# Per-layer embedding of the first token tile placed between the row lookups of the second tile

## What is computed

```python
def peer_ffn(h, ...):              # per token: 8 heads x 16 picked rows of u_tab and v_tab
    act = jax.nn.gelu(jnp.einsum('cd,ckd->ck', xc, uc))
    return jnp.einsum('ck,ckd->cd', gc * act, vc)

def per_layer_embed(h, p_i, g, w_gate, w_proj):
    gate = jax.nn.sigmoid(rms_norm(h, g) @ w_gate)      # w_gate 1024 x 1024
    return h + gate * (p_i @ w_proj)                    # p_i 256 tokens x 256, w_proj 256 x 1024

# layer i:
h = h + peer_ffn(rms_norm(h, norm_ffn[i]), ...)
h = per_layer_embed(h, p[i], norm_ple[i], ple_w_gate[i], ple_w_proj[i])
```

## Time and profile before

| | us |
|---|---|
| median of 3 runs | 3167.94 |
| lowest and highest run | 3167.43, 3169.96 |
| the profiled execution: its own time | 3172.68 |
| its span, first to last instruction | 3170.8 |
| first row loop, first lookup issued to last matmul | 186.0 to 863.8 |
| end of it to the first kv matmul | 863.8 to 923.3 |
| second row loop's last matmul to the first mix_in matmul | 1810.3 to 1879.3 |

### The profile page before, as it was taken

One profiled execution on the slowest core, in us unless ns is written; L12 is line 12 of the kernel. 1 busy time (PEld: TensorE's weight loads), 2 busy tenths in 40 slices (PEclk: granted clock), 3 DMA queues, 4 the chain that ended last, 5 costly groups with the idle time before them and its releaser, 6 DMA issues.

```text
span 3170.8 us, 28409 instructions
## 1 busy us (share of the span) xinstructions
PE 2703.6 (85%) x9642; PEld 1254.1 (40%) x9642; DVE 1345.4 (42%) x3325; ACT 581.9 (18%) x1216; POOL 487.8 (15%) x526
## 2 busy tenths in 40 slices
PE   8898777777788898777877789669999999999998
PEld 7373333333355473333333346534333333333233
DVE  3547777776521547777776420333111111111112
ACT  1112222222102312222222101301111111111111
POOL 0014333333200014333333100000000000000000
PEclk9799998999889999999899989578999999999999
DMA  4679999999625479999999623043999999899987
GB/s 173 241 288 410 421 421 421 422 421 421 287 93 186 173 303 420 421 421 421 421 421 421 261 93 143 17 167 160 385 422 422 422 422 422 353 422 422 422 362 302
DMA packets 145580, 1049.89 MB, mean 331 GB/s; under 512 B 16304, under 2 KB 16560, under 8 KB 18512
## 3 DMA queue, kind: packets, MB, share of 16 engines
q0 software_dynamic: 74064, 537.56, 40.8%
q1 hardware_dynamic: 70560, 508.59, 39.5%
q10 hardware_dynamic: 864, 2.65, 0.2%
HBM read 1047.69 MB, written 1.05 MB: 331 GB/s over the span
## 4 chain that ended last, share of the span: by engine, by line
PE 51%; DMA 37%; DVE 7%; ACT 2%; issue 1%; DVEq 1%; SPq 0%; POOL 0%; ACTq 0%; POOLq 0%
DMA big<-in_peer_uv,rows_of 20%; DMA big<-in_moe 12%; PE psum L526 11%; PE psum L806 10%; PE psum L426 9%; PE psum L438 7%; PE psum L832 5%; DMA uv_more<-in_peer_uv,rows_of 4%; DVE big L1305 2%; PE psum L721 1%; PE psum L787 1%; PE psum L800 1%; PE psum L473 1%; DMA ring<-in_ada 1%; ACT gdiag L914 1%
## 5 line engine op out<-in xcount | busy, mean ns | idle before, releaser
L526 PE MATMUL psum<-big,gdiag 128*128 128x512 f32 x1880 | 923.7, 648 | 275.3 <-ACT gdiag L914 275.3
L1305 DVE CUSTOM_DVE_ANT_0 big<-psum,big 128x1024 f32<-128x1024 f32 x470 | 575.0, 1224 | 312.8 <-DMA big<-in_peer_uv,rows_of 308.1
L526 PEld LDWEIGHTS psum<-big,gdiag 128*128 128x128 f32 x1880 | 377.9, 207 | 818.0 <-issue 442.3
L1669 POOL DMA_INDIRECT big<-in_peer_uv,rows_of x470 | 443.1, 943 | 1262.5 <-PE psum L526 762.2
L806 PE MATMUL psum<-big 128*64 128x512 f32 x2240 | 501.1, 597 | 25.0 <-POOLq L1691 24.5
L1635 DVE TENSOR_SCALAR big<-psum 128x512 f32<-128x512 f32 x35 | 24.2, 692 | 663.0 <-PE psum L806 663.0
L806 PEld LDWEIGHTS psum<-big 128*64 128x64 f32 x2240 | 152.6, 137 | 371.0 <-issue 276.6
L426 PE MATMUL psum<-big,ring 128*128 128x256 f32 x1280 | 288.8, 389 | 9.3 <-DVE big L1130 3.4
L426 PEld LDWEIGHTS psum<-big,ring 128*128 128x128 f32 x1280 | 250.0, 196 | 47.7 <-DVE big L1130 4.3
L832 PE MATMUL psum<-ring,big 128*64 128x512 f32 x1120 | 248.1, 595 | 3.9
L438 PE MATMUL psum<-ring,big 128*128 128x512 f32 x480 | 216.8, 614 | 3.3 <-DVE big L1130 2.3
(11 more groups left out here) (347 smaller groups left out, 1828.5 us busy)
## 6 DMA issues: line engine op xcount, KB each, us to landing
big<-in_moe SPq DMA_DIRECT2D x256, 1024.0 KB, 20.6
ring<-in_moe SPq DMA_DIRECT2D x128, 1024.0 KB, 19.6
ring<-in_ada SPq DMA_DIRECT2D x24, 1024.0 KB, 7.4
ring<-in_peer_wq SPq DMA_DIRECT2D x16, 1024.0 KB, 7.2
ring<-in_mix_in SPq DMA_DIRECT2D x14, 1024.0 KB, 6.2
ring<-in_a_in SPq DMA_DIRECT2D x8, 1024.0 KB, 7.4
ring<-in_ple_gate SPq DMA_DIRECT2D x8, 1024.0 KB, 9.0
ring<-in_kv SPq DMA_DIRECT2D x8, 1024.0 KB, 6.2
```

Of the source, the lines that this page charges most:

```text
L526: mm = pe.matmul(psum[:, OUT_BANK[t] + c, :], gdiag[:, n % DIAGS, :], uv[(PICKS * l + n) % ROWS][:, D + c * 512:D + (c + 1) * 512], start= ...
L1305: j = dve.tensor_tensor_reduce(out=u, in0=x, in1=u, scale=1.0, scalar=0.0, op0=ALU.mult, op1=ALU.add, accum_out=dots[:, n:n + 1])
L1669: pool.indirect_dma_start(uv[g % ROWS], None, table, bass.IndirectOffsetOnAxis(rows_of[:, n:n + 1], 0)).then_inc(uv_loaded[g % ROWS], 16)
```

## The change

For tile 0 the whole per-layer embedding is done while the rows of tile 1 are looked up. On VectorE it is a generator, `first_tile`, of which one step is taken after every fourth pick from n = 139 on, with pauses (a `yield 9` leaves eight groups of four picks out). On TensorE and ScalarE its pieces stand at fixed picks. Scratch for it lies in parts of `big` that hold the top-k scores and queries until then. `ple_proj` leaves the ring; its weights and `pT` are loaded by SP into SBUF as soon as the last product of the queries is done. Only tile 1 is left behind the loop. The row of the final norm moves from the diagonals' buffer to `big`, and is spread at pick 180.

```diff
-    ("ple_gate0", 2, "AA"), ("ple_proj0", 1, "DDDD"),
+    ("ple_gate0", 2, "A"),
...
@@ SyncE: peer(l)
-                load(FIRST[f"ple_proj{l}"], d["ple_proj"][l], words=2 * D)
+                sp.wait_ge(tile_done, ENDS[FIRST[f"peer_q{l}"] + 3])
+                sp.dma_start(proj_w, d["ple_proj"][l].rearrange("p (k f) -> p k f", k=2)).then_inc(p_loaded, 16)
+                sp.dma_start(pT, d["pT"][l]).then_inc(p_loaded, 16)
...
@@ TensorE: peer(l, i)
+                def gate_first(s):
+                    pe.wait_ge(xT_ready, 4 * (i + 1) + 4 * l + 2)
+                    for k in range(KC):
+                        mm = pe.matmul(psum[:, 6 + s, :], xT[:, k, 0:P], w[:, k, :], start=(k == 0), stop=(k == KC - 1))
+                    mm.then_inc(gate0_done, 1)
+                def project(t):
+                    for c in range(2):
+                        for k in range(2):
+                            mm = pe.matmul(psum[:, 4 + c, :], pT[:, k, t * P:(t + 1) * P],
+                                           proj_w[:, k, c * 512:(c + 1) * 512], start=(k == 0), stop=(k == 1))
+                    mm.then_inc(prod_done, 1)
                 for n in range(BATCH, PICKS):
+                    if n == 148:
+                        turn(i + 1, first, (0,))
+                    if n == 156:
+                        gate_first(0)
+                    if n == 164:
+                        gate_first(1)
+                    if n == 176:
+                        pe.wait_ge(p_loaded, 32 * (l + 1))
+                        project(0)
+                    if n == 180 and l:
+                        pe.wait_ge(gate0_ready, 4)
+                        for half in range(2):
+                            spread(half, V8("final_norm"), half, 6 + half)
+                    if n == 212:
+                        pe.wait_ge(prod_taken, 2 * l + 1)
+                        project(1)
                     mix_rows(n)
@@ TensorE: ple(l, i): tile 1 alone
+                turn(i, hs, (1,))
...
+                        mm = pe.matmul(psum[:, m % 3, :], xT[:, k, P:T], w[:, k, :], start=(k == 0), stop=(k == KC - 1))
...
+                pe.wait_ge(prod_taken, 2 * l + 2)
...
+            turn(3, first, (0,))
+            turn(3, hs, (1,))
@@ ScalarE: row loop, and behind it
+                        if at == 136:
+                            root(4 + 6 * l, 0)
+                        if at == 168:
+                            for s in range(2):
+                                act.wait_ge(gate0_done, 2 * l + s + 1)
+                                act.activation(gate0[:, s * 512:(s + 1) * 512], psum[:, 6 + s, :],
+                                               ACT.Sigmoid).then_inc(gate0_ready, 1)
+                        if at == 184:
+                            root(5 + 6 * l, 0)
+                            if l:
+                                for half in range(2):
+                                    take_row(half, row_f, half, 6 + half)
+                        if at == 188 and l:
+                            root(12, 0)
...
-                act.dma_start(pT, d["pT"][l]).then_inc(p_loaded, 16)
                 act.dma_start(late, d["late"]).then_inc(late_loaded, 16)
@@ VectorE: peer(l, i)
+                def first_tile():
+                    dve.wait_ge(v_done, PICKS * l + PICKS // TT)
+                    for c in range(2):
+                        o = h[:, 0, c * 512:(c + 1) * 512]
+                        dve.tensor_tensor(o, o, psum[:, OUT_BANK[0] + c, :], ALU.add)
+                    dve.drain()
+                    square(0, h[:, 0, :], first[:, 0, :])
+                    yield 1
+                    inverse(4 + 6 * l, 0)
+                    scaled(0, first)
+                    yield 2
+                    gains(i + 1, V8(f"norm_ple{l}"), tiles=(0,))
+                    yield 9
+                    dve.wait_ge(gate0_ready, 2 * l + 2)
+                    dve.wait_ge(prod_done, 2 * l + 1)
+                    o = gate0.rearrange("p (a b) -> p a b", a=2)
+                    dve.tensor_tensor(o, psum[:, 4:6, :], o, ALU.mult).then_inc(prod_taken, 1)
+                    dve.drain()
+                    dve.tensor_tensor(h[:, 0, :], h[:, 0, :], gate0, ALU.add)
+                    dve.drain()
+                    square(0, h[:, 0, :], first[:, 0, :])
+                    yield 1
+                    inverse(5 + 6 * l, 0)
+                    if l:
+                        dve.wait_ge(row_taken, 2)
+                        dve.scalar_tensor_tensor(h[:, 0, :], h[:, 0, :], rstd[:, 0:1], row_f, ALU.mult, ALU.mult)
+                        dve.drain()
+                        square(0, h[:, 0, :], first[:, 0, :])
+                        yield 1
+                        inverse(12, 0)
+                    scaled(0, first)
+                    yield 99
...
+                            if n >= 139:
+                                pause -= 1
+                                if pause <= 0:
+                                    pause = next(beside)
+                dve.wait_ge(v_done, PICKS * (l + 1))
+                for c in range(2):
+                    o = h[:, 1, c * 512:(c + 1) * 512]
+                    dve.tensor_tensor(o, o, psum[:, OUT_BANK[1] + c, :], ALU.add)
+                dve.drain()
+                square(1, h[:, 1, :])
+                inverse(6 + 7 * l, 1)
+                scaled(1)
```

More of the change, by code:

```diff
@@ L190, in build @@
         ple_t = region(4096, TT, D)
-        pT = region(6144, 2, T)
+        proj_w = region(24576, 2, D)
+        pT = region(26624, 2, T)
+        gate0 = region(27136, D)
+        first = region(28672, 1, D)
         xT2 = region(2048, KC, T)
@@ L440, in tokens, with turn @@
                     mm.then_inc(tile_done, 1)
-            def turn(i, src=hs):
-                for t in range(TT):
-                    pe.wait_ge(hs_ready, 2 * i + t + 1)
+            rows_made = {2: (5, 7), 3: (6, 8), 5: (11, 13), 6: (12, 14)}
+            def turn(i, src=hs, tiles=(0, 1)):
+                for t in tiles:
+                    pe.wait_ge(hs_ready, rows_made[i][t] if i in rows_made else 2 * i + t + 1)
                     for b in range(2):
@@ L450, in turn, with spread @@
                         mm.then_inc(turned, 1)
-            def spread(n, vec, half):
-                if n:
+            def spread(n, vec, half, bank=3):
+                if n > 2:
                     pe.wait_ge(row_taken, n)
                 for k in range(4):
-                    mm = pe.matmul(psum[:, 3, k * P:(k + 1) * P],
+                    mm = pe.matmul(psum[:, bank, k * P:(k + 1) * P],
                                    vec[:, 4 * half + k:4 * half + k + 1].to_broadcast([P, P]), ident,
@@ L635, in _ @@
             pe.wait_ge(late_loaded, 32)
-            turn(6)
+            turn(6, first, (0,))
+            turn(6, hs, (1,))
             pe.wait_ge(xT_ready, 32)
@@ L856, in roots, with take_row @@
                     root(2 * i + t, t)
-            def take_row(n, row, half):
+            def take_row(n, row, half, bank=3):
                 act.wait_ge(row_done, n + 1)
-                act.activation(row[:, half * 512:(half + 1) * 512], psum[:, 3, :], ACT.Copy).then_inc(row_taken, 1)
+                act.activation(row[:, half * 512:(half + 1) * 512], psum[:, bank, :], ACT.Copy).then_inc(row_taken, 1)
             def two(x):
@@ L933, in peer, with ple @@
                             batch(at)
+                        if at == 136:
[12 more added lines that the diff above has]
+                            root(12, 0)
                     if p + 2 < PAIRS:
                         exponents(p + 2)
-            def ple(l, i):
+            def ple(l):
                 act.wait_ge(v_done, PICKS * (l + 1))
-                act.dma_start(pT, d["pT"][l]).then_inc(p_loaded, 16)
                 act.dma_start(late, d["late"]).then_inc(late_loaded, 16)
-                if l:
-                    for half in range(2):
-                        take_row(half, row_f, half)
-                roots(i)
+                root(6 + 7 * l, 1)
                 m = tile0(f"ple_gate{l}")
-                for g in range(4):
-                    act.activation(gate_sb[:, g % 2, (g // 2) * 512:(g // 2 + 1) * 512], tile_in(m + g),
+                for g in range(2):
+                    act.activation(gate_sb[:, 1, g * 512:(g + 1) * 512], tile_in(m + g),
                                    ACT.Sigmoid).then_inc(act_took, 1)
             peer(0, 1)
-            ple(0, 2)
-            roots(3)
+            ple(0)
+            root(7, 1)
             m = tile0("kv")
@@ L980, in _ @@
             peer(1, 4)
-            ple(1, 5)
-            for n in range(12, 16):
-                root(n, n // 2 - 6)
+            ple(1)
+            for n in range(14, 16):
+                root(n, 1)
             m = tile0("mix_in")
@@ L1114, in normed, with gains @@
                 scaled(t)
-            def gains(i, gain, gain2=None, shift=None):
-                for t in range(TT):
```

(23 more changed lines are left out.)

59 lines of the change are left out of this document (13 added, 46 removed).

## The result

| | before | after |
|---|---|---|
| median of 4 runs, us | 3167.68 | 3120.96 |
| lowest and highest run | 3166.21, 3169.96 | 3119.94, 3122.31 |
| the profiled execution: its own time | 3172.68 | 3121.47 |
| its span | 3170.8 | 3119.6 |

The ratio is 0.9846, 95% interval 0.9834 to 0.9857: 46.7 us, or 1.5%, faster. The forecast was 3118.0 in a range of 3107 to 3137.

A forecast was written before the change was run, and what follows sets the result against it. DMA bytes were taken to bound the row loops, a serial chain the tails behind them. Tails 56.0 us shorter minus 6.2 for loads gave 49.8 less: 3122.9 against the profiled execution, 3118 against the median, range 3107 to 3137.

The forecast's parts named there:

- The tails: From last row matmul to next stage: 59.5 to 34.4 us in layer 0, 69.0 to 38.1 in layer 1.
- Steps 1, 4, 5 and 6: Tile 1's tail: add-to-transpose 4.27 us; last sigmoid, hand-over 0.65; product-to-scaling 4.10/7.47; scaling-to-next-stage matmul 5.59/5.91.
- Step 3: Tile 1's gate products in the tail: two groups instead of four, 10.17 plus 6.86, together 17.03 us.
- The cover of the root's table: Start of the tail: ScalarE's 1.28 us table load ends before the squares are ready, so it costs nothing.
- The loads: Projection weights and pT moved into the row loop, 1.31 MB a layer: 3.1 us each, 6.2 in all.
- The work in the loop at nothing: Tile 0's work inserted in the row loops costs nothing, covered by 10.0 us of queued lookups.
- VectorE's lump after pick 187: Row loop: the largest inserted VectorE piece, 4.0 us, followed after pick 191 by 3.1 in layer 1.
- The loop goes at the pace of bytes: Row loops: DMA bytes at 420 GB/s set the pace, 2.50 us a pick, 10.0 for four.
- hidden loads: Rival: the loads moved into the row loop cost nothing, 3112 us; chance 0.08.
- A delay partly passed on: Rival: the lookup queue covers only part of the row loop's delay, 3131 us at half, 3144 in full; chance 0.08.
- Full payment of the inserted work: Rival: the row buffers run dry after each inserted piece, 46 us back, 3164 us; chance 0.04.
- a slower clock of TensorE: Rival: the kernel gets slower through TensorE's clock; chance 0.04.

The follow-up runs named there:

- after_again: The changed kernel run and profiled a second time, nothing altered, on another chip: median 3119.5 us, ratio 0.9827, tails 34.2 and 37.1 us.
- before_again: The kernel before, profiled a second time, nothing altered: row loops 613.6 and 614.2 us, tails 59.2 and 69.1 us.
- tail_warm: Changed kernel with tile 0's gains and transposes drawn into the tail's gate groups, plus idle matmuls in TensorE's tail: 3112.7 us, ratio 0.9807.
- no_loads: Changed kernel without the row loop's loads of projection weights and pT: loops 612.6 and 613.2 us; median 3131.1 us, with 36 MoE blocks instead of 35.
- before_loads: Kernel before, with unread copies of projection weights and pT also loaded in the row loop: 3175.6 us, ratio 1.0026; loops 616.1 and 616.4 us.
- light_gate: Changed kernel with one of eight products left in each tile 0 gate group: loops 617.3 and 617.8 us; median 3096.1 us, with 34 MoE blocks.
- gates_together: Changed kernel with both tile 0 gate groups ahead of pick 156, 13.7 us in one piece: ratio 0.9843, loops 616.4 and 616.1 us.
- gates_x2: Changed kernel with both tile 0 gate groups ahead of pick 156, each computed twice, 27.4 us: ratio 0.9916, loops 628.3 and 629.3 us.
- code_dve: Changed kernel with four drain instructions behind each dot product on VectorE: 3141.0 us, ratio 0.9902, loops 624.4 and 624.6 us.

## Why the prediction was right

1. *The tails.* 25.1 and 30.9 us were forecast, 26.3 and 31.9 measured (25.0 and 32.0 with after_again and before_again). Steps 1, 4, 5 and 6 came out within 0.05 us of their prices (step 6: 897.22 - 891.63 = 5.59, and 1825.18 - 1819.27 = 5.91). The tails are 1.2 and 1.0 us shorter than the 34.4 and 38.1 of the sum because the first gate group, priced at 10.17, took 880.04 - 870.97 = 9.07 and 9.82, and in layer 1 the transposes took 1.34 instead of 1.97 us. That is the moment at which the clock rises: in the first 4 us of the group 0.50 was granted in before and 0.52 in after, in the next 4 us 0.74 and 1.00. The figure isn't fixed: over all kernels with after's tails the first group took 8.6 to 10.2 us, so how near it came is in part chance. Step 3 was right to keep this cost whole and not to halve it with the dense stretch: two groups are left of four, and the first still took 9.07 and 9.82. tail_warm shows its cause: the clock was 0.50 after 4.2 us of standing, with the fill it was 1.00, and both groups together took 14.00 us instead of 15.90.
2. *The cover of the root's table.* The load ends at 864.40 + 1.28 = 865.68 and the root waits for VectorE until 866.93, so it stayed covered. In the kernel before, where nothing else held the root up, it ran 1.30 us after the load's start (864.66), so the trace's 1.28 stands:

```profile
865.96 0.20 ACT L852 ACTIVATE std<-ms 128x1 f32<-128x1 f32 x1
```

3. *The loads.* 3.1 us a layer forecast. Measured 2.7 and 2.5 between the two kernels (2.8 and 2.1 between their second profiles), 3.3 and 2.8 by no_loads, 2.8 and 2.9 by before_loads. The choice of the upper end was right, and the argument too.
4. *The work in the loop at nothing.* Right, and tested from both sides by light_gate and gates_together. The term behind it was mis-sized: the slack is 11.8 to 13.4 us, not the 10.0 of 15.6 - 5.6. That difference reads the queueing of whole rows, while what counts may be how far the slowest DMA engine is behind; no run shows that by itself. Some 6 us of bytes could be lost for nothing in gates_together and gates_x2; 4 to 6 dot products had come about 1 us late by then. That these two are the same thing fits in size, and wasn't tested by itself. Two smaller readings were off without harm: VectorE's lump after pick 187 puts 5.68 us between two dot products instead of 2.48, so it delays by 3.2, not 4.0; and the 8.83 us read for a group of four picks is the last group of the loop, which took 7.13 in after, as a settled one does in before (at 704.19).
5. *"The loop goes at the pace of bytes."* Too coarse. As I infer from the 25 to 29 GB/s behind the loop and from the 8.4 and 8.6 us of code_dve, it goes at the pace of one DMA engine, through which VectorE's program also comes. From pick 130 to 255 are 125 steps of 2.48 us, 310.0, and five late dot products of 1.0 us: 315, where 315.3 to 315.5 were taken, in before and in after. It changed nothing in the sum, since both kernels have five of them there by the landing events.
6. *The net.* 49.8 us forecast, 46.7 between the medians, 51.2 between the profiled executions, 54.8 on another chip. Loops and tails, the two things that the sum is made of, give -53.0 by the table, 3.2 more than forecast. The +3.0 in mix_in, which repeats and which the sum doesn't have, takes most of that back, so the net is nearer to the forecast than its terms are, and that is luck. The rest is in stages where the same kernel differs from itself by 3 to 4 us, and between chips; it isn't explained further.

Of the rivals, hidden loads fall by three runs. A delay partly passed on falls for the change as made and appears in gates_x2, a piece twice as long. Full payment of the inserted work doesn't show, the loops being 2.7 and 2.5 us longer, nor does a slower clock of TensorE: 0.93 was granted from 250 to 845 us in before and in after.

## What to carry to other kernels

Work that stands in a serial tail can be put into a stage that waits for DMA, and what decided here was the longest single piece, less the spare time of the groups it stands in, against the queueing that the lookups carry: 13.7 us in one piece were free, 27.4 cost 12 to 13. Bytes moved into such a stage were paid for in every run: 1.31 MB cost 2.1 to 3.3 us a layer, where their size at 420 GB/s gives 3.1. After shortening a serial chain, look at TensorE's granted clock in it: it was 0.50 here, and a few idle matmuls ahead of the first real ones and behind the gates brought 1.00 and took 6.0 us off two tails.

## What the hardware did that was not expected

- One DMA engine of 16 seems to set the pace of the lookups. That is inferred from the rate behind the loop (25 to 29 GB/s, a sixteenth of 421 being 26), the late landings (3.46 us after the one before instead of 2.48) and the two code runs (8.4 and 8.6 us longer against 0.3 and 0.2 shorter); no row names the engine. By the code runs VectorE's program comes through it. Behind an 8 KB packet of q14 a row landed 1.0 us late once the loop had settled, though the packet itself is a small part of that, 0.7% of 16 engines' time over 3 us, or 0.3 us on one. Where the other 0.7 us go is open.
- Instructions that do nothing cost time in this loop on VectorE: 1024 more for each loop made it 8.4 and 8.6 us longer; on ScalarE they made it no longer (615.6 and 615.8 against 615.9 and 616.0).
- At the end of a loop the rate stands at 25 to 29 instead of 421 GB/s for 8 us, and the dot products still wait for rows, 1.2 us each.
